# A fused three-block transformer kernel: its large SBUF buffers moved to another offset modulo 512 bytes

## The reference

```python
def expert_block(args):                      # 32 experts, w_gate_up 1024 x 2048, w_down 1024 x 1024
    idx, e = args
    xb = xpad[idx]
    gu = xb @ w_gate_up[e] + b_gate_up[e]
    x_glu = jnp.minimum(gu[:, ::2], SWIGLU_LIMIT)
    x_lin = jnp.clip(gu[:, 1::2], -SWIGLU_LIMIT, SWIGLU_LIMIT)
    act = x_glu * jax.nn.sigmoid(SWIGLU_ALPHA * x_glu) * (x_lin + 1.0)
    return act @ w_down[e] + b_down[e]

def swiglu(x, w1, w3, w2):                   # four times, inner width 2816
    return (jax.nn.silu(x @ w1) * (x @ w3)) @ w2
```

## Time and profile before

| | |
|---|---|
| median of three runs | 2844.82 us |
| the profiled execution, from first to last instruction | 2848.0 us |
| TensorE busy | 2735.0 us, 96% |
| VectorE busy | 2059.4 us, 72% |
| ScalarE busy | 1627.8 us, 57% |
| moved by DMA | 700.34 MB |

### The profile page before, as it was taken

How to read it: one execution, slowest core, us unless ns; L and a number is a source line. 1 busy time by engine, 2 the same in 40 slices (tenths; PEclk the granted TensorE clock), 3 DMA queues, 4 the chain that set the end, 5 groups by cost and what they waited for, 6 DMA issues and landing times.

```text
span 2848.0 us, 38484 instructions
## 1 busy us (share of the span) xinstructions
PE 2735.0 (96%) x12282; PEld 2160.9 (76%) x12282; DVE 2059.4 (72%) x2438; ACT 1627.8 (57%) x2055; POOL 209.0 (7%) x213
## 2 busy tenths in 40 slices
PE   8997999999999999999999999989999999989999
PEld 5654888888888888888868877777787787867787
DVE  4655999999999999999964567765545555877544
ACT  2322888888888888888844435434344344345443
POOL 0002111111111111111100000000000000200000
PEclk9997999999999999999999999999999999999999
DMA  8745999999999999999955654254456456534554
GB/s 314 249 150 194 353 354 351 351 353 357 358 359 355 355 358 353 354 352 351 352 190 182 197 166 150 97 179 154 147 181 210 133 177 199 167 104 143 160 182 143
DMA packets 263482, 700.34 MB, mean 246 GB/s; under 512 B 29512, under 2 KB 128240, under 8 KB 213680
## 3 DMA queue, kind: packets, MB, share of 16 engines
q1 hardware_dynamic: 249780, 685.19, 68.2%
q0 software_dynamic: 9504, 8.42, 1.0%
q10 hardware_dynamic: 4124, 5.77, 0.6%
HBM read 706.57 MB, written 23.63 MB: 256 GB/s over the span
## 4 chain that ended last, share of the span: by engine, by line
PE 86%; DVE 6%; issue 2%; DMA 2%; ACT 2%; SPq 1%; POOL 1%; POOLq 0%; DVEq 0%; ACTq 0%
PE bank L664 23%; PE bank L666 22%; PE bank L665 22%; PE bank L1175 3%; PE bank L1173 3%; PE bank L1174 3%; PE bank L790 1%; PE bank L814 1%; DMA raw<-in_w_in 1%; PE bank L1046 1%; PE bank L1012 1%; PE bank L1072 1%; PE bank L838 1%; PE bank L738 1%; PE bank L756 1%
## 5 line engine op out<-in xcount | busy, mean ns | idle before, releaser
L664 PE MATMUL bank<-w_hi,HTh 128*128 128x512 f32 x2824 | 1134.4, 402 | 17.1 <-DVE HTl L1368 9.5
L666 PE MATMUL bank<-w_hi,HTl 128*128 128x512 f32 x2824 | 1117.3, 396 | 0.0
L665 PE MATMUL bank<-w_lo,HTh 128*128 128x512 f32 x2824 | 1116.7, 395 | 0.0
L1317 DVE TENSOR_TENSOR w_lo<-raw,w_hi 128x1024 fp32r<-128x1024 f32 (+3 forms) x406 | 482.7, 1214 | 273.2 <-ACT w_hi L2293 270.0
L2293 ACT ACTIVATE w_hi<-raw 128x1024 fp32r<-128x1024 f32 (+3 forms) x406 | 420.3, 1052 | 436.2 <-PE bank L666 283.8
L664 PEld LDWEIGHTS bank<-w_hi,HTh 128*128 128x128 f32 x2824 | 533.3, 189 | 148.8 <-DVE HTl L1368 13.8
L666 PEld LDWEIGHTS bank<-w_hi,HTl 128*128 128x128 f32 x2824 | 532.7, 189 | 126.9
L665 PEld LDWEIGHTS bank<-w_lo,HTh 128*128 128x128 f32 x2824 | 533.6, 189 | 115.5
L1964 DVE TENSOR_TENSOR w_lo<-arena,w_hi 128x1024 fp32r<-128x1024 f32 x256 | 316.2, 1235 | 44.5 <-ACT w_hi L2491 44.5
L1964 DVE TENSOR_TENSOR w_lo<-raw,w_hi 128x1024 fp32r<-128x1024 f32 x256 | 298.7, 1217 | 5.4 <-ACT w_hi L2536 3.6
L2491 ACT ACTIVATE w_hi<-raw 128x1024 fp32r<-128x1024 f32 x252 | 266.9, 1059 | 59.2 <-PE bank L666 59.2
(11 more groups left out here) (365 smaller groups left out, 2678.6 us busy)
## 6 DMA issues: line engine op xcount, KB each, us to landing
raw<-in_moe_w SPq DMA_DIRECT2D x128, 1024.0 KB, 5.1
arena<-in_moe_w SPq DMA_DIRECT2D x128, 1024.0 KB, 4.9
H<-in_moe_w SPq DMA_DIRECT2D x64, 1024.0 KB, 5.4
MIX<-in_moe_w SPq DMA_DIRECT2D x64, 1024.0 KB
raw<-in_ffn_w SPq DMA_DIRECT2D x248, 256.0 KB, 3.3
raw<-in_ffn_w_gu SPq DMA_DIRECT2D x164, 256.0 KB, 3.3
raw<-in_w_in SPq DMA_DIRECT2D x76, 512.0 KB, 4.6
raw<-in_ffn_w_down SPq DMA_DIRECT2D x80, 256.0 KB, 3.5
```

The source lines that it names most:

```text
L664: pe.matmul(acc, xh, wh, start=start, stop=False)
L665: pe.matmul(acc, xh, wl, start=False, stop=False)
L666: return pe.matmul(acc, xl, wh, start=False, stop=stop)
L1317: dve.tensor_tensor(lo_at(n, c), raw_at(n, c), hi_at(n, c).bitcast(F32), ALU.subtract).then_inc(lo_done, 1)
```

## The change

A buffer `pad` of 32 bytes on each partition is declared ahead of `raw`, and `arena` and `arena_r` grow from 10888 to 11008 elements, by 480 bytes. Nothing reads or writes the added bytes.

```diff
+        sb("pad", [P, 8])
         raw = sb("raw", [P, RAW, TILE])
         w_hi = sb("w_hi", [P, PARTS, TILE], F32R)
         w_lo = sb("w_lo", [P, PARTS, TILE], F32R)
         with ExitStack() as shared:
-            arena_r = shared.enter_context(nc.sbuf_tensor("arena_r", [P, 10888], F32R))
-        arena = sb("arena", [P, 10888])
+            arena_r = shared.enter_context(nc.sbuf_tensor("arena_r", [P, 11008], F32R))
+        arena = sb("arena", [P, 11008])
         X = sb("X", [P, TT, D])
```

## The result

The changed kernel takes 2804.11 us (median of four runs, 2802.07 to 2806.09) against 2845.4 us for four runs of the kernel before: a ratio of 0.9849, with a 95% interval of 0.9837 to 0.9862, or 41 us less. The forecast was 2794 us, with 2784 to 2846 us for eight times in ten. Of the 22 executions of the kernel before that were taken beside the first four experiments one took 9501 us; it is left out of the ratios. In the profiled executions the span falls from 2848.0 to 2800.3 us, 47.7 us.

The account below looks back on a forecast made before the run. TensorE, busy for 96% of the span, was taken as the bound: matmuls times their start distance. Experts' 25.6 plus the rest's 24.9 us made 50.5, from 2848.0 to 2797.5, less 3.2 for the median: 2794 us; range 2784 to 2846.

Parts of the forecast that it names:

- the odd stretches of `arena_r`: Two of six stretches of `arena_r`, at 416 and 432 after the change: matmuls reading them would stay at 233 ns.
- The experts' term: Mixture of experts: 148 matmuls save 0.87 us of 36.26, less VectorE's hold-ups; 0.80 us by 32 experts, 25.6 us.
- eight matmuls of settling: In each expert, after each of four transpose groups: 32 matmuls save 3.3 ns, the other 116 save 6.6 ns.
- the waits for `w_lo`: In each expert, two weight loads wait for VectorE's `w_lo`: 0.05 and 0.02 us taken from the gain.
- the wait at 601.59: Expert's already late tile, weight load waiting 0.20 us for `w_lo`: savings of twelve matmuls beside it become wait, 0.05 us.
- the wait at 619.03: Expert's second weight load, waiting 0.15 us without delaying a matmul yet: charged 0.02 us.
- The rest's term: Outside the experts: 4620 matmuls save 6.0 ns each, 27.7 us, nine tenths on the path (bounds 0.75 and 1): 24.9 us.
- the forecast's own range: Whole kernel, if the remainder counts and about 50 us is gained: 2784 to 2812 us; chance 0.75.
- What was costed at nothing: VectorE's subtractions, DMA landings up to 0.5 us later, demand at 362 GB/s, transposes, narrow and plain float32 matmuls: no time.
- Nothing changes: Rival: the remainder is not the cause, place in SBUF could be; `w_hi` stays at 233.3 ns, 2845 us; chance 0.11.
- Slower by DMA writes at 32 modulo 64: Rival: loads into `raw` and `arena` cost the DMA engines more; at 15% per piece, 2872 us; chance 0.06.
- That the experts don't take the gain: Rival: VectorE's tight places or DMA at 0.97 become waits; experts give 8 us or none, 2812 or 2820 us; chance 0.08.

Follow-up runs that it names:

- w160_ht128: Changed kernel with an arena 32 bytes shorter: weights stay at 160 modulo 512, `HTh`, `extra` and all behind them at 128; 2844.9 us, 0.9993 of the kernel before.
- all128: Changed kernel without `pad`, keeping the longer arena: weights, `HTh` and all behind them at 128 modulo 512; 2801.0 us, 0.983 of the kernel before.

## Why the prediction was right, and where it was off

*The mechanism.* Right: the distance between 512-column fp32r matmuls falls from 233.3 to 226.7 ns in long runs. The prediction left open whether 160 is good or a shared remainder; it is the shared one, and, as far as the stretch at 416 shows, it is modulo 256, not 512. That is why its one claim from reading `arena_r` fell: "the odd stretches of `arena_r`, then at 416 and 432, still at 233". 416 differs from 160 by 256 and runs at 226.7; 432, a difference of 16, runs at 231.6 on the mean of its twelve matmuls.

*The experts' term, 0.80 us by 32.* Measured: 36.27 to 35.67, 0.593 us, or 19.0 us in all against 25.6. The working had 0.87 less 0.07, and both parts were mis-sized. Between the two kernels with VectorE's new order, in which nearly no stall is left, an expert falls from 36.24 to 35.53, 0.71 us, against the 0.87. On the mean of 28 rounds, 140 of the 148 matmuls fall from 233.1 ns to 228.0. The prediction's eight matmuls of settling at 230.0 come to a mean of 233.3 - 5.9 = 227.4 ns; the settling is longer (ten matmuls with a mean of 231), which is 140 x 0.6 = 0.08 us; the start was 233.1 and not 233.3 (0.03 us); and the other eight, the one ahead of and the one behind each group of transposes, save nothing (8 x 5.9 = 0.05 us). From the 0.71 the waits for `w_lo` take 0.12 where 0.07 was charged. The stalls themselves add up to the 0.07, though not where they were charged: the one behind the wait at 601.59 grew by only 14 ns (265 - 233 = 32 before, 46 after; 50 was charged), and the wait at 619.03 came to delay a matmul by 58 ns (20 was charged). The other 0.05 is that each stall also breaks the rhythm for some matmuls, which the prediction didn't count. 0.16 and 0.05 are the 0.21 us that are missing.

*The rest's term, 24.9 us.* By the profiled spans the rest gives 47.7 - 19.0 = 28.7 us; by the medians of the runs 41.3 - 19.0 = 22.3. The 24.9 lies between. The steps of the four feed-forward networks, by 40 of their 44, take 682.6 us before and 665.9 after: 16.7 us for 2832 matmuls, 5.9 ns each where 6.0 was said, so this part is wholly on the path. The spans differ by 6.4 us more than the medians do. The profile after is of the fastest of its four runs (2802.07 us), and the one before holds a stretch at a low clock: from the last step of the third network to the first of the fourth it takes 263.3 us at a granted clock of 0.95, where `w160_ht128`, with matmuls as slow, takes 258.0 us at 0.97, and the changed kernel 258.4 us at 0.97. So some 5 of the 28.7 us are the clock, and in this stretch, with its attentions, the shorter distance doesn't show in the time. That is the step that was sized too high: of the 27.7 us nine tenths were put on the path, and by the medians it is 22.3/27.7 = 0.8, within the bounds of 0.75 and 1. Single executions of the kernel before scatter from 2841.8 to 2853.2 us on one chip, with the granted clock between 0.985 and 0.979.

*The sum.* 50.5 us was forecast and 41.3 came: 6.6 of the missing 9.2 are the experts' term, 2.6 the rest's by the medians. Both terms missed the same way, so nothing cancelled; the 2804 us lie within the forecast's own range of 2784 to 2812 us because it allowed for longer settling and for a smaller share on the path.

*What was costed at nothing.* VectorE's subtractions 1221 against 1217 ns, ScalarE busy 1624 against 1628 us, DMA at a share of 0.96 with no tile that ScalarE waits for: as said. The demand rose to 359 GB/s, not 362, since the experts got faster by less.

*The rivals.* Nothing changes: its reason was the place in SBUF, and the pair of `all128` and `w160_ht128` refutes that. The Trainium skill, page "SBUF — State Buffer", section "Who interferes with whom", calls TensorE's two read ports independent. That is not borne out here: the same matmuls of the same shape take 226.7 or 233.3 ns by where one operand lies against the other. Its other sentence, that PE never waits on anyone, is about other engines, and these runs don't speak against it. Slower by DMA writes at 32 modulo 64: nothing of it is seen in the time, since `raw` and `arena` at 160 or at 128 (`all128`, 2801.0 us) come to the same, nor in the packets, which take 0.309 us where 10% more on eight loads of twelve would make it 0.331. The time from issue to landing is less clear. In `all128`, at the changed kernel's pace but with everything at 128, it is

```profile
arena<-in_moe_w SPq DMA_DIRECT2D x128, 1024.0 KB, 5.2
H<-in_moe_w SPq DMA_DIRECT2D x64, 1024.0 KB, 5.5
```

against 6.8 and 6.9 us after the change, yet `w160_ht128`, at 160 and the slow pace, has 4.8 in `arena`. So neither the address alone nor the pace alone explains the later landings, and one profile each doesn't settle it; in the experts TensorE doesn't wait for them. That the experts don't take the gain: a quarter of it is missing, but of those 6.6 us the waits that this rival named make only 32 x 0.05 = 1.6 beyond what was charged; the rest is settling and the start at 233.1. No wait for the DMA engines came in the experts.

## What to carry to other kernels

Where TensorE is busy all the time, read the distance between the starts of equal matmuls whose operands lie in different buffers; two levels in one trace are a lever that costs no instruction. In this kernel's form, fp32r matmuls of 512 columns at 2.4 GHz with a weight load for each, let moving and stationary operands begin at the same remainder modulo 256 bytes, all of a stream and not most of it, and then clear the small stalls, because each one also costs the settling behind it. And a scan that changes a setting every few instructions measures the mixture where the matmuls take ten to settle.

## What the runs showed of the hardware

The distance between 512-column fp32r matmuls at 2.4 GHz ("warm") depends on the two operands' addresses: 226.7 ns at a difference of 0, and in short runs of 256, 231.6 at 16 in a few matmuls, 233 at 32, 229 at 64, 232 to 233 at 128 and 233 at 192 and 224. The Trainium skill, page "TensorE: Matmul & The Clock Gate", section "Wait — 56ns, not 53.3ns?", has the columns by 2.4 GHz and 2.5 ns, which is 215.8 ns, and no run here came down to it. At 1.2 GHz nothing is gained, as the earlier trace rows showed. After the change, three matmuls there:

```profile
1634.67 0.63 PE L665 MATMUL bank<-extra,HTh 128*128 128x512 f32 x1
1635.10 0.63 PE L666 MATMUL bank<-extra,HTh 128*128 128x512 f32 x1
...
1635.95 0.63 PE L665 MATMUL bank<-extra,HTh 128*128 128x512 f32 x1
```

(1635.95 - 1634.67) / 3 = 427 ns. The fast pace is reached only after some ten matmuls: in the changed kernel the distances behind a group of transposes are, again and again, 315 ns and then 235, 234, 236, 224, 231, 235, 229, 232, 231, then 227. Why the places of the two operands matter at all, and why 64 above differs from 64 below, no run here can show; it stays open.
